# The query's operand rounded chunk by chunk into a home of its own, and the first picks turned some rows sooner

## What is computed

```python
h = h + conformer_conv(rmsnorm(h, a_norm_g[i]), ...)        # layer 0, ends in u @ w2 + b2
h = h + diff_attention(rmsnorm(h, b_norm_g[j]), ...)        # layer 1, ends in o @ wo
h = h + peer(rmsnorm(h, f_norm_g[layer]), f_wq[layer], ...) # both layers

def chunk(xc):                                  # peer, 128 tokens
    q = (xc @ wq).reshape(PEER_CHUNK, PEER_HEADS, 2, PEER_HALF)
    s1 = jnp.einsum('chd,kd->chk', q[:, :, 0], sk1)
    s2 = jnp.einsum('chd,kd->chk', q[:, :, 1], sk2)
    v1, i1 = lax.top_k(s1, PEER_TOPK)
    v2, i2 = lax.top_k(s2, PEER_TOPK)
    ...                                         # top 16 of the sums, their experts
    gate = jax.nn.softmax(top_s.astype(jnp.float32), axis=-1).astype(xc.dtype)
    act = jax.nn.gelu(jnp.einsum('cd,chkd->chk', xc, u_tab[expert]), approximate=False)
    return jnp.einsum('chk,chkd->cd', gate * act, v_tab[expert])
```

## Time and profile before

| | |
|---|---|
| median of 3 timed runs | 2810.82 us (2805.54 to 2812.44) |
| the profiled execution | 2802.38 us |
| its span, first to last instruction | 2800.6 us |
| TensorE matmul busy | 2706.8 us, 97% of the span |
| VectorE busy | 2033.5 us, 73% |
| ScalarE busy | 1510.7 us, 54% |
| GpSimd busy | 615.6 us, 22% |
| mean granted TensorE clock | 0.988 |

### The profile page before, as it was taken

How to read it: one execution, slowest core, us unless ns; L and a number is a source line. 1 busy time by engine, 2 the same in 40 slices (tenths; PEclk the granted TensorE clock), 3 DMA queues, 4 the chain that set the end, 5 groups by cost and what they waited for, 6 DMA issues and landing times.

```text
span 2800.6 us, 60626 instructions
## 1 busy us (share of the span) xinstructions
PE 2706.8 (97%) x21599; PEld 2607.8 (93%) x21599; DVE 2033.5 (73%) x4480; ACT 1510.7 (54%) x3277; POOL 615.6 (22%) x659
## 2 busy tenths in 40 slices
PE   9999999999999998999999999999998899998998
PEld 8899889999999997889899999999987799987998
DVE  7759988787787865779888777777676665556665
ACT  7453355555555554652455555555545655556554
POOL 1033680021111213125850010010044300022000
PEclk9999999999999999999999999999999999999999
DMA  5055427787887843256347677676643046532564
GB/s 182 7 168 175 128 74 248 228 293 248 266 269 245 291 146 117 64 167 201 99 139 233 223 238 237 224 239 221 188 136 125 21 155 186 180 126 78 159 194 135
DMA packets 153654, 493.92 MB, mean 176 GB/s; under 512 B 18033, under 2 KB 37937, under 8 KB 153489
## 3 DMA queue, kind: packets, MB, share of 16 engines
q1 hardware_dynamic: 137424, 437.67, 48.0%
q0 software_dynamic: 15488, 54.11, 6.8%
q10 hardware_dynamic: 576, 0.03, 0.0%
HBM read 481.62 MB, written 10.13 MB: 176 GB/s over the span
## 4 chain that ended last, share of the span: by engine, by line
PE 87%; DVE 8%; ACT 2%; issue 1%; POOL 1%; DMA 0%; POOLq 0%; DVEq 0%; ACTq 0%
PE banks L841 67%; PE banks L1085 7%; PE banks L1244 2%; PE banks L1106 2%; PE banks L983 2%; DVE meta_row L2343 1%; DVE work L2346 1%; PE banks L879 1%; PE banks L874 1%; POOL x_lo L2841 1%; DVE w_lo L545 1%; ACT w_hi L538 1%; DVE arena L2326 1%; PE banks L1361 0%; DVE att_small L2633 0%
## 5 line engine op out<-in xcount | busy, mean ns | idle before, releaser
L545 DVE TENSOR_TENSOR w_lo<-ring,w_hi 128x512 fp32r<-128x512 f32 x1448 | 1014.0, 704 | 551.2 <-ACT w_hi L538 527.2
L538 ACT ACTIVATE w_hi<-ring 128x512 fp32r<-128x512 f32 x1448 | 908.9, 630 | 756.0 <-PE banks L841 710.2
L841 PE MATMUL banks<-gated_all,w_hi 128*128 128x240 f32 (+1 forms) x5120 | 886.2, 278 | 6.4 <-DVE gated_all L2410 6.4
L841 PE MATMUL banks<-x_hi,w_hi 128*128 128x240 f32 (+2 forms) x3008 | 853.2, 284 | 22.5 <-POOL x_lo L2841 7.2
L841 PE MATMUL banks<-x_lo,w_hi 128*128 128x240 f32 (+2 forms) x3008 | 843.7, 280 | 0.0
L841 PE MATMUL banks<-x_hi,w_lo 128*128 128x240 f32 (+2 forms) x3008 | 839.2, 279 | 0.0
L841 PEld LDWEIGHTS banks<-gated_all,w_hi 128*128 128x128 f32 x5120 | 776.5, 190 | 8.3 <-DVE gated_all L2410 8.3
L841 PE MATMUL banks<-gated_all,w_lo 128*128 128x240 f32 (+1 forms) x2560 | 706.9, 276 | 0.0
L841 PEld LDWEIGHTS banks<-x_hi,w_hi 128*128 128x128 f32 x3008 | 572.6, 190 | 36.0 <-issue 13.9
L841 PEld LDWEIGHTS banks<-x_hi,w_lo 128*128 128x128 f32 x3008 | 574.0, 191 | 0.0
L841 PEld LDWEIGHTS banks<-x_lo,w_hi 128*128 128x128 f32 x3008 | 572.4, 190 | 0.5
(11 more groups left out here) (369 smaller groups left out, 2835.2 us busy)
## 6 DMA issues: line engine op xcount, KB each, us to landing
ring<-in_peer_v SPq DMA_DIRECT2D x256, 512.0 KB, 3.6
ring<-in_peer_u SPq DMA_DIRECT2D x184, 512.0 KB, 4.5
arena<-in_peer_u SPq DMA_DIRECT2D x72, 512.0 KB, 3.7
ring<-in_mlp_up SPq DMA_DIRECT2D x64, 512.0 KB, 3.5
ring<-in_mlp_down SPq DMA_DIRECT2D x64, 512.0 KB, 3.5
ring<-w_peer_query SPq DMA_DIRECT2D x32, 512.0 KB, 3.5
ring<-w_fox_proj SPq DMA_DIRECT2D x24, 512.0 KB, 3.5
ring<-w_nsa_proj SPq DMA_DIRECT2D x20, 512.0 KB, 3.5
```

Source lines behind the costliest of these rows:

```text
L538: act.activation(w_hi[:, hn % SPLITS], raw_half(hn), ACT.Copy).then_inc(hi_ready, 1)
L545: dve.tensor_tensor(w_lo[:, hn % SPLITS], raw_half(hn), w_hi[:, hn % SPLITS].bitcast(F32), ALU.subtract)\
L841: mm = pe.matmul(out, w_at(w), x, start=start and j == 0, stop=stop and j == 2, skip_group_check=True)
```

## The change

The rounded part and the remainder of the query's operand go to two new tiles, `xq_hi` and `xq_lo`, in the arena. ScalarE rounds chunk m-2 in step m of `proj_add`, ahead of its square, and the last two chunks in `norm_added`, which no longer waits for `half_used`. VectorE takes the remainder of chunk m-3 in steps 3 to 7 and of chunks 5 to 7 behind them. `peer_query` reads the new tiles. In `peer_select` the first turn and the store of the first picks stand behind early row 22 in layer 0 and row 21 in layer 1 (`FIRST_TURN`), and the third tile's exponential (layer 0 only) ahead of row 21.

```diff
-EXPS_BEFORE = {11: 0, 19: 1}
+EXPS_BEFORE = {11: 0, 19: 1, 21: 2}
+FIRST_TURN = (EARLY_FIRST - 2, EARLY_FIRST - 3)
...
+        xq_at = ev.at - 2 * NC * X_STEP
+        xq_at -= (arena_from + 4 * xq_at - MOVED_AT + 4 * META) % ROW // 4
...
+        xq_hi, xq_lo = rounded("xq_hi", xq_at, NC, X_STEP), rounded("xq_lo", xq_at + NC * X_STEP, NC, X_STEP)
...
-            def project(n, bank, tokens, i=None, x_run=None, parts=None, s={}, beside=None):
+            def project(n, bank, tokens, i=None, x_run=None, parts=None, s={}, beside=None, xs=(x_hi, x_lo)):
...
-                                   x_hi[:, cc_, tk_], x_lo[:, cc_, tk_], cc_ == 0, cc_ == NC - 1)
+                                   xs[0][:, cc_, tk_], xs[1][:, cc_, tk_], cc_ == 0, cc_ == NC - 1)
...
-                            beside=spread_in_middle if m == 2 else None)
+                            beside=spread_in_middle if m == 2 else None, xs=(xq_hi, xq_lo))
...
-                turn(0)
+                    if k == FIRST_TURN[s["layer"]]:
+                        turn(0)
...
                         act.wait_ge(bank_free, s["bf0"] + m - 1)
+                        round_raw(stages[s["at"] + 1], m - 2)
                         square(squares[:, m - 2, tk_], h[:, m - 2, tk_])
...
+            def round_raw(s, c):
+                tk_ = tok_slice(s["tokens"])
+                act.activation(xq_hi[:, c, x_slice(s["tokens"], s)], h[:, c, tk_], ACT.Copy, scale=vec(s["gain"], s["gi"], c))\
+                   .then_inc(x_hi_ready, 1)
+
             def norm_added(s):
                 added, tk_ = stages[s["at"] - 1], tok_slice(s["tokens"])
-                act.wait_ge(half_used, 2 * (added["n0"] + NC))
-                for c in range(NC):
-                    if c >= NC - 2:
-                        act.wait_ge(bank_free, added["bf0"] + c + 1)
-                    act.activation(x_hi[:, c, x_slice(s["tokens"], s)], h[:, c, tk_], ACT.Copy, scale=vec(s["gain"], s["gi"], c))\
-                       .then_inc(x_hi_ready, 1)
+                for c in (NC - 2, NC - 1):
+                    act.wait_ge(bank_free, added["bf0"] + c + 1)
+                    round_raw(s, c)
...
                 for k in range(EARLY_FIRST):
-                    if k in EXPS_BEFORE:
+                    if EXPS_BEFORE.get(k, len(tiles)) < len(tiles):
                         exps(EXPS_BEFORE[k])
                     early(k)
+                    if k == FIRST_TURN[s["layer"]]:
+                        store_picks(0)
...
-                if len(tiles) > NT:
-                    exps(NT)
-                store_picks(0)
...
-            def rest_of_raw(s):
+            def rest_of_raw(s, part):
...
-                for c in range(NC):
+                for c in part:
...
-                    rest_of_raw(s)
+                    rest_of_raw(s, range(NC - 3, NC))
...
                     ins.then_inc(bank_free, 1)
+                    if m >= 3:
+                        rest_of_raw(stages[s["at"] + 1], [m - 3])
```

More of the change, by code:

```diff
@@ L2115, in invert_wide @@
                 return banks[:, 5, 0:T0]
-            def rest_of_raw(s):
+            def rest_of_raw(s, part):
                 tk_, x_at = tok_slice(s["tokens"]), x_slice(s["tokens"], s)
-                for c in range(NC):
+                for c in part:
                     dve.wait_ge(x_hi_ready, NC * s["x0"] + c + 1)
-                    dve.scalar_tensor_tensor(out=x_lo[:, c, x_at], in0=h[:, c, tk_], scalar=vec(s["gain"], s["gi"], c),
-                                             in1=x_hi[:, c, x_at].bitcast(F32), op0=ALU.mult, op1=ALU.subtract)\
+                    dve.scalar_tensor_tensor(out=xq_lo[:, c, x_at], in0=h[:, c, tk_], scalar=vec(s["gain"], s["gi"], c),
+                                             in1=xq_hi[:, c, x_at].bitcast(F32), op0=ALU.mult, op1=ALU.subtract)\
                        .then_inc(x_lo_ready, 1)
```

## The result

The changed kernel takes 2782.72 us in the median of five runs (2777.35 to 2791.91); the kernel before, run between them, 2805.54 us (2798.24 to 2812.44). The ratio is 0.9924, 95% interval [0.9903, 0.9945]. Faster, as forecast, but by 23 us and not by 12, and under the lower end of the range. The profiled execution took 2781.11 us, span 2779.3, against 2802.38 and 2800.6 before: 21.3 us less.

The account below looks back on a forecast made before the run. TensorE was taken to bound the kernel, at 87% of the chain; 2.55 + 1.16 + 6.2 + 2.15 = 12.1 us off the median 2810.8 gave 2798.7 us, range 2790 to 2807.

Parts of the forecast that it names:

- What bounds the kernel: TensorE carries 87% of the chain; an edit is worth what it removes of TensorE's idle time, slow stretches or VectorE waits.
- Part 1, layer 0: Border from projection to query: four chunks less of VectorE's pace, 1.25 us net, plus 1.3 us of slow clock, 2.55 us.
- Part 1, layer 1: Same border in layer 1: 1.58 us gained less 0.42 for GpSimd's later addition, 1.16 us.
- The cover of the added work: Projection steps: added roundings and remainders fit idle time, weight halves keep some 2.5 us of cover, so cost nothing.
- Part 2: Layer 0's early rows to group loop: 3.2 us idle plus 3.1 slow clock, less 0.1 loop waits, 6.2 us.
- Rival B: The clock comes out otherwise, so 4.4 us of slow stretches are not gained: 7.7 us, 2803.1 us; chance 0.24.
- Part 3: Layer 1's turn two rows sooner: 1.55 us idle time goes, plus 0.6 of loop waits, 2.15 us.
- The sum: All gains together 12.1 us: 2790.3 from the profiled run, 2798.7 against the median of three, 2810.8.
- How the numbers follow: Forecast chance 0.62; about 0.3% (8.4 us) distinguishable from no change; faster 0.70, same 0.26, slower 0.04; range allows 2 us scatter above.
- C: Picks come behind the earlier turn or VectorE's own work holds the loop: only 5.8 us gained, 2805.0 us; chance 0.08.
- D: Slower: rounding within projection steps makes weight halves late, 21.6 us lost less the 12.1 gained, 2820.3 us; chance 0.06.
- What would make it wrong: Signs against: idle TensorE inside the projections, a wait ahead of the turn (L1095), or new stretches at 0.50 elsewhere.

Follow-up runs that it names:

- before again: The kernel before, run again with no edit: ratio 1.0008 [0.9989, 1.0028].
- whole third: The whole change once more, unedited, on another chip, beside 35 runs of the kernel before: ratio 0.9962 [0.9944, 0.9979].
- exponential late: Against the changed kernel, layer 0's third exponential put back behind the last early row, the turn still early: one run, 2785.69 us.
- remainder and square early: Changed kernel with chunk 4's remainder ahead of the last addition and weight half, and ScalarE's sixth square ahead of its last rounding: 0.9956 against before, median 2782.73 us.
- single parts: Query operand's new home alone, 0.9988 and again 0.9987; moved turns and exponential alone, 0.9990 and again 0.9978; all against the kernel before.

## Why the prediction was wrong, point by point

**What bounds the kernel: right.** TensorE carries 85% of the chain now, VectorE 10% (87 and 8). What the edits gave came out of TensorE's idle time, its slow stretches and its waits for VectorE at the two kinds of place named.

**Part 1, layer 0, 2.55 us: right.** The border took 18.0 us in every kernel without the edit and 15.3 in every one with it (less where chunk 4 comes sooner still): 2.7. Its terms hold: chunks 0 to 3 lie in the old gap, chunk 4 comes when chunk 0 came, GpSimd's addition costs the 0.4 us (0.88 against 0.49, ending 0.30 behind it), and the slow clock is gone. The Trainium skill's rule taken whole ("SBUF — State Buffer", section "Who interferes with whom") would have let it end its full 0.49 us behind the addition; here too it ended 0.30 behind, so the measurement decides against the rule's full length and for the blocking itself.

**Part 1, layer 1, 1.16 us: right.** 12.0 to 10.7 or 10.9 us, so 1.1 to 1.3; 2.8 where the clock had dropped behind the old gap.

**The cover of the added work: right.** No weight half was late; the 32 us of projection ahead of the border in layer 0 took 31.73 us before and 31.81 after, the 40 in layer 1 39.89 and 39.80.

**Part 2, 6.2 us: right for the trace it was made on, too large for the kernel.** Against that trace the border gave 67.89 - 61.57 = 6.3 us. The mean of the four executions without the edit is (67.89 + 65.89 + 65.35 + 65.35) / 4 = 66.1, that of the five with the turns edited and nothing else new 61.9: 4.3 us. The 3.2 us of idle time went in every one, but the slow clock, counted at 3.1 us, was there in one execution of four, and where it was the border was 2.0 to 2.5 us longer (67.89 against 65.35 to 65.89). Rival B named that term as the doubtful one, and for this border it was nearer.

**Part 3, 2.15 us: right.** 56.87 to 54.59 in every pair: 2.3.

**The sum, 12.1 us: right, within its uncertainty.** The four borders gave 12.7 against the first trace; by the means over all executions 2.7 + 1.65 + 4.3 + 2.3 = 10.9 (layer 1's query at 12.38 without the edit, one of the four at 13.52, and 10.73 with it). The whole change's two series of twelve runs gave 13.0 and 8.5, mean 10.7.

**The steps that failed** are the anchor in "Sum" and the scatter in "How the numbers follow". The 12.1 us were taken off the median of three runs, 2810.8. That median was 9 to 13 us too high for this kernel: the runs beside the experiments, 35, 35 and 17 of them, have theirs at 2797.9, 2798.0 and 2801.9. The prediction had the sign before it, a profiled run 8.4 us under the median; it had 2790.3 from that run and moved up to 2798.7. From 2798 the same sum gives 2786, inside the five measured runs. And the range allowed 2 us of scatter each way, where runs of one and the same kernel lie 19 to 26 us apart. The profile of before held the reason: its two MLPs are the same 1440 matmuls, and one takes 169.88 us, the other 163.48, neither with idle time in it. I read the stages that the diff touches and no others, and so never saw that. Of the 21.3 us between the two traces, 12.7 are the edits, 12.0 are two such loops that fell short in the one and long in the other, and -3.4 lie in stretches between that no edit touches. Of the 23 us between the medians, about 11 are the change. Some 3 more are the five runs of the changed kernel, whose mean, 2783.7, lies under those of the two later series, 2785.2 and 2788.7. The other 8 are the five runs of before, with a mean of 2806.0 against 2797 to 2800 in the three later series. Five runs that scatter as these series do have a mean good to 2.5 us, so that this was the draw alone is not likely; what else made them long, no run shows.

**Where the 3.4 us went.** 1.8 us of them lie in a stretch of 250 us behind layer 1's dense loop, 1.9 between the two MLPs; the rest gave 0.3 back. What made the second stretch longer stays open. In the first the clock differs, and the prediction did not look there either. Windows, first over that stretch (before, then changed), then behind one and the same matmul, which starts at 2105.47 us before and at 2084.63 in the changed kernel, both times after 2.00 us of idle time:
```profile
2017.00:2267.00 250.00, 222.50 (x1754) 206.13 (x1753) 165.61 (x350) 142.70 (x373) 94.36 (x118) 0.96 0.31 100
1998.00:2250.00 252.00, 225.93 (x1758) 210.11 (x1756) 166.05 (x351) 142.84 (x372) 93.23 (x118) 0.94 0.32 99
...
2105.00:2107.00 2.00, 1.53 (x13) 1.56 (x14) 0.36 (x1) 0.42 (x1) 1.92 (x4) 1.00 0.72 186
2085.00:2087.00 2.00, 2.00 (x11) 2.00 (x11) 0.00 (x0) 0.00 (x0) 1.86 (x5) 0.50 0.58 217
```
By the granted clock TensorE spent about 20 us of the stretch at 0.50 before and 31 in the changed kernel, and the stretch took 251.0 and 252.8 us. Over the twelve executions of the table the two go together: where the slow time sums to 17 to 21 us (before, before again, whole third, exponential late, remainder and square early) the stretch took 248.3 to 251.1, where it sums to 27 to 34 (the other seven) 252.8 to 257.2. Both executions of before stand in the first group and all four of the single parts in the second, but the whole change stands in either; so it scatters by itself, and whether the edits have a hand in it too, twelve executions don't settle.

**The rivals.** B's 2803.1 lies further off than the forecast. Its mechanism, a slow stretch that the kernel before does not always have, was real at layer 0's turn (absent in three executions of four) and not at layer 0's query (there in all four). C did not come about: both turns took their idle time away whole, layer 0 with 1.75 us of VectorE's work to spare. D did not either.

**What would make it wrong** listed idle TensorE inside the projections and a wait ahead of the turn, which did not appear, and new stretches at 0.50 elsewhere, which did, as just shown: the stretch that holds them grew by 1.8 us, which did not undo the sum. It did not list a loop untouched by the diff taking another time.

## What to carry to other kernels

Before working out a sum, compare stages of the trace that run the same code: if two of them differ with no idle time in either, the next execution may have it the other way round, as here by 6.4 us in each MLP, and both the range and the worth of a single median have to follow. Judge a small edit by the time between the same two numbered instructions across its own border, in several executions: here, where the clock was the same, that repeated within 0.2 us at three borders and 0.6 at the fourth, where twelve timed runs left 2 us open. A term that hangs on the clock behind a short gap is a chance and not a size: count it at how often it is seen, not whole.

## What the runs showed of the hardware

- **Two distances between matmuls.** Back-to-back matmuls of 240 columns start every 112.0 or 113.3 ns (4200 of them in 470.67 or 476.26 us), those of 256 columns every 113.3 or 117.7 ns (1440 in 163.5 or 169.9 us), at the full granted clock and without idle time. A piece of equal matmuls kept one of the two throughout (60 loops, and the pieces between stops); from one piece to the next it could change, behind a stop of TensorE and also behind 16 matmuls of 16 columns without any idle time. The five long loops of this kernel come to 1268.4 us if all are short and 1292.4 if all are long, by the table (the 1263 and 1287 in one expectation were added up wrongly). What settles it stays open, and whether a kernel could steer it was not tried.
- **The clock behind a gap.** After 2.52 us idle ahead of layer 0's query it fell to 0.50 in all four executions that have this gap; after 3.19 us ahead of layer 0's groups in one of four; after 2.46 us ahead of layer 1's query in one of four; after the 3.52 us with the exponential late in the one execution there is; after the 1.55 us ahead of layer 1's groups in none of four; after the 1.29 to 1.37 us left by the change in none. After 2.00 us behind layer 1's dense loop the same matmul of the same stage found it at 1.00 in one trace and at 0.50 in another.
- **VectorE beside GpSimd.** A remainder of 0.49 us took 0.88 with GpSimd's addition beside it, ending 0.30 us behind it. The addition itself took 0.76 us there, and 1.43 and 0.99 us in the two versions where remainders were already running when it began.
